# One layer of a hybrid decoder on one core: the first expert's tokens are gathered in turned form, between its first units

## The reference, cut to what matters

```
h   = rms_norm(x, ffn_norm_g)                      # 256 tokens x 1024
top_logit, top_e = top_k(h @ router_w + router_b, 4)
for each expert e:                                 # its tokens only
    gu  = xb @ w_gate_up[e] + b_gate_up[e]         # 1024 -> 2 x 1024
    act = glu * sigmoid(1.702 * glu) * (lin + 1)   # clamped at 7
    y   = act @ w_down[e] + b_down[e]              # 1024 -> 1024
x   = x + sum over e of gate * y
out = rms_norm(x, final_norm_g)
```

## Time and profile before

| | |
|---|---|
| median of three runs | 1133.32 us |
| the profiled execution, its own time | 1133.06 us |
| its span, first to last instruction | 1131.3 us |
| what lies around the span | 1.76 us |
| TensorE busy | 1083.2 us (96%) |
| DVE busy | 281.0 us (25%) |
| ACT busy | 164.9 us (15%) |
| bytes read from HBM | 430.32 MB |
| granted TensorE clock, mean | 0.998 |

### The profile page before, as it was taken

One profiled execution on the slowest core, in us unless ns is written; L12 is line 12 of the kernel. 1 busy time (PEld: TensorE's weight loads), 2 busy tenths in 40 slices (PEclk: granted clock), 3 DMA queues, 4 the chain that ended last, 5 costly groups with the idle time before them and its releaser, 6 DMA issues.

```text
span 1131.3 us, 13266 instructions
## 1 busy us (share of the span) xinstructions
PE 1083.2 (96%) x5094; PEld 466.3 (41%) x5094; DVE 281.0 (25%) x662; ACT 164.9 (15%) x347; POOL 10.2 (1%) x28
## 2 busy tenths in 40 slices
PE   7999999999999999999999999999999999999996
PEld 5578777543333333333333333333333333333333
DVE  2055532233222222222222222221111111222212
ACT  2144450210000000011000101000000000000002
POOL 0101000000000000000000000000000000000000
PEclk9999999999999999999999999999999999999999
DMA  9923652879999999999999999999999999999996
GB/s 319 332 88 149 231 216 102 353 297 419 430 431 431 431 431 432 430 432 430 433 430 433 430 433 430 432 431 432 431 431 432 430 432 430 432 430 433 430 417 266
DMA packets 47013, 431.67 MB, mean 382 GB/s; under 512 B 6256, under 2 KB 8688, under 8 KB 23408
## 3 DMA queue, kind: packets, MB, share of 16 engines
q1 hardware_dynamic: 46848, 431.12, 90.8%
q10 hardware_dynamic: 144, 0.26, 0.1%
HBM read 430.32 MB, written 1.05 MB: 381 GB/s over the span
## 4 chain that ended last, share of the span: by engine, by line
PE 59%; DMA 19%; SPq 17%; DVE 2%; issue 1%; ACT 1%; ACTq 0%
PE bank L936 23%; DMA raw<-in_w_gate_up 17%; PE bank L955 10%; PE bank L568 7%; SPq L458 7%; SPq L519 5%; SPq L461 5%; PE bank L601 4%; PE bank L572 4%; PE bank L903 3%; PE bank L870 3%; PE bank L817 2%; DMA raw<-in_w_down 1%; PE bank L622 1%; PE bank L835 0%
## 5 line engine op out<-in xcount | busy, mean ns | idle before, releaser
L936 PE MATMUL bank<-raw,xT 128*64 128x512 f32 x2048 | 462.1, 597 | 26.3 <-DMA raw<-in_w_gate_up 24.3
L936 PEld LDWEIGHTS bank<-raw,xT 128*64 128x64 f32 x2048 | 139.2, 137 | 320.6 <-issue 256.3
L955 PE MATMUL bank<-raw,actT 128*64 128x512 f32 x992 | 225.7, 596 | 0.7 <-DMA raw<-in_w_down 0.5
L955 PEld LDWEIGHTS bank<-raw,actT 128*64 128x64 f32 x992 | 68.2, 137 | 129.6 <-issue 117.1
L1555 DVE TENSOR_SCALAR gated<-cst,posc,gates 128x128 f32<-128x128 f32 x64 | 19.3, 343 | 276.4 <-PE bank L903 276.4
L1589 DVE TENSOR_TENSOR gub<-bank,bias_gu 128x512 f32<-128x512 f32 x64 | 43.9, 685 | 166.4 <-PE bank L572 166.4
L1596 DVE COPY ev_gu<-bank 128x512 f32<-128x512 f32 x32 | 22.1, 692 | 221.9 <-PE bank L936 221.9
L1221 ACT COPY ev_gu<-bank 128x512 f32<-128x512 f32 x32 | 18.7, 585 | 389.4 <-PE bank L936 389.4
L903 PE MATMUL bank<-ev,gated 64*128 64x512 f32 x248 | 61.6, 615 | 0.0
L870 PE MATMUL bank<-x_res,onehot 128*64 128x512 f32 x256 | 60.4, 592 | 0.0
L568 PE MATMUL bank<-hT,front_raw 128*128 128x256 f32 x256 | 58.9, 383 | 0.0
(11 more groups left out here) (243 smaller groups left out, 587.3 us busy)
## 6 DMA issues: line engine op xcount, KB each, us to landing
raw<-in_w_gate_up SPq DMA_DIRECT2D x124, 2048.0 KB, 41.9
raw<-in_w_down SPq DMA_DIRECT2D x60, 2048.0 KB, 43.8
front_raw<-in_w_in SPq DMA_DIRECT2D x6, 2048.0 KB, 13.8
raw<-in_w_gate_up SPq DMA_DIRECT2D x16, 512.0 KB, 17.5
raw<-in_w_down SPq DMA_DIRECT2D x16, 512.0 KB, 14.9
front_raw<-in_w_out SPq DMA_DIRECT2D x2, 2048.0 KB, 9.6
front_raw<-in_w_branch_mla SPq DMA_DIRECT2D x1, 2048.0 KB, 7.9
front_raw<-in_w_branch_dsa SPq DMA_DIRECT2D x1, 2048.0 KB, 7.9
```

Source lines behind the costliest of these rows:

```text
L936: mm = pe.matmul(GU[pair][half * SLOTS:(half + 1) * SLOTS, :], xT[:, c, b, :], w[:, at:at + BLK], start=u == 0 and k == 0, stop=last and k ...
L955: mm = pe.matmul(DN[half * SLOTS:(half + 1) * SLOTS, :], actT[:, c, u, :], w[:, at:at + BLK], start=u == 0 and c == 0, stop=u == DN_UNITS ...
```

## The change

Item 0's tokens are no longer gathered and turned. The function `first_tokens(u)` takes `xs`, with every fourth feature, as stationary operand (128 tokens x 128 features) and `onehot` as moving operand (128 tokens x 64 slots). The result has features on partitions at once. There are four groups, one for each gate-up unit, each with two chunks of 128 features and, for each, two matmuls (one a block of tokens). Each group has its own bank: 6, 3, 0 and 1. DVE multiplies each group by its part of the gain into `xT`: four instructions of 128 x 128 in place of one of 128 x 512. Groups 0 and 1 run before unit 0, group 2 between units 0 and 1, group 3 between units 1 and 2. ACT's copy of item 0's tokens, its four transposes, and the four `stay_warm` matmuls behind them are gone. TensorE's register load of `n_items` moves from before item 0 to behind item 0's last down unit, ahead of item 2. Items 1 and on are gathered as before; the counts of `gath_ps`, `gath_ev`, `xT_ps` and `xT_ok` start one lower.

```
@@ banks
+        FIRST = (B[6], B[3], B[0], B[1])
@@ TensorE
+            def first_tokens(u):
+                b, c0 = u // 2, 2 * (u % 2)
+                for k in range(2):
+                    for t in range(TT):
+                        a = b * BLK + c0 + k
+                        mm = pe.matmul(FIRST[u][:, k * SLOTS:(k + 1) * SLOTS], xs[:, t, a:a + BLK - c0 - k:4],
+                                       onehot[:, t, :], start=t == 0, stop=t == TT - 1)
+                mm.then_inc(first_ps, 1)
...
             stay_warm(WARM[2])
             pe.wait_ge(hot_ok, 1)
-            gather()
-            turn_tokens(0)
-            stay_warm(WARM[3])
-            pe.wait_ge(n_ok, 1)
-            pairs = pe.value_load(n_items[0:1, 1:2], ...) + 2
+            first_tokens(0)
+            first_tokens(1)
...
-                if u == 0:
-                    pe.wait_ge(xT_ok, i + 1)
-                    if not first:
-                        pe.wait_ge(bias_ok, 2 * i)
+                if first:
+                    pe.wait_ge(first_ok, u + 1)
+                elif u == 0:
+                    pe.wait_ge(xT_ok, i)
+                    pe.wait_ge(bias_ok, 2 * i)
...
             for u in range(GU_UNITS):
                 gate_up(0, 0, u)
+                if u < 2:
+                    first_tokens(u + 2)
...
             down(0, 0, 1)
+            pe.wait_ge(n_ok, 1)
+            pairs = pe.value_load(n_items[0:1, 1:2], ...) + 2
@@ ScalarE
-            tokens_out(0)
@@ VectorE
-            tokens_in(0)
+            for u in range(GU_UNITS):
+                b, c0 = u // 2, 2 * (u % 2)
+                dve.wait_ge(first_ps, u + 1)
+                dve.tensor_tensor(xT[:, c0:c0 + 2, b, :], FIRST[u][:, 0:2 * SLOTS].rearrange("p (c s) -> p c s", c=2),
+                                  g_tok[:, b, c0:c0 + 2].unsqueeze(2).to_broadcast([P, 2, SLOTS]), ALU.mult).then_inc(first_ok, 1)
...
             def next_tokens(i):
-                dve.wait_ge(gath_ps, i + 1)
+                if isinstance(i, int) and i == 0:
+                    dve.wait_ge(first_ps, GU_UNITS)
+                else:
+                    dve.wait_ge(gath_ps, i)
                 pick_tokens(i + 1)
```

More of the change, by code:

```diff
@@ L310, in build @@
         xT_ok = sem("xT_ok")
+        first_ps = sem("first_ps")
+        first_ok = sem("first_ok")
         sc_ps = sem("sc_ps")
@@ L872, in gather @@
                 mm.then_inc(gath_ps, 1)
+            def first_tokens(u):
[6 more added lines that the diff above has]
+                mm.then_inc(first_ps, 1)
             def turn_tokens(i):
-                pe.wait_ge(gath_ev, i + 1)
+                pe.wait_ge(gath_ev, i)
                 for c in range(4):
@@ L882, in _ @@
             pe.wait_ge(hot_ok, 1)
-            gather()
-            turn_tokens(0)
-            stay_warm(WARM[3])
-            pe.wait_ge(n_ok, 1)
-            pairs = pe.value_load(n_items[0:1, 1:2], min_val=EXPERTS // 2 - 2, max_val=EXPERTS * CHUNKS // 2 - 2) + 2
+            first_tokens(0)
+            first_tokens(1)
             def turn_scatter(i):
@@ L1018, in _ @@
             down(0, 0, 1)
+            pe.wait_ge(n_ok, 1)
+            pairs = pe.value_load(n_items[0:1, 1:2], min_val=EXPERTS // 2 - 2, max_val=EXPERTS * CHUNKS // 2 - 2) + 2
             pe.wait_ge(x1_in, 2 * TT)
@@ L1202, in tokens_out @@
             def tokens_out(i):
-                act.wait_ge(gath_ps, i + 1)
+                act.wait_ge(gath_ps, i)
                 act.copy(ev[:, :], PREP[:, :]).then_inc(gath_ev, 1)
-            tokens_out(0)
             act.wait_ge(n_ok, 1)
@@ L1572, in next_tokens @@
             def next_tokens(i):
-                dve.wait_ge(gath_ps, i + 1)
+                if isinstance(i, int) and i == 0:
+                    dve.wait_ge(first_ps, GU_UNITS)
+                else:
+                    dve.wait_ge(gath_ps, i)
                 pick_tokens(i + 1)
             def tokens_in(i):
-                dve.wait_ge(xT_ps, i + 1)
+                dve.wait_ge(xT_ps, i)
                 dve.tensor_tensor(xT[:, :, :, :], PREP[:, :].rearrange("p (c h s) -> p c h s", c=4, h=2),
```

## The result

The changed kernel is slower: median 1138.55 us of seven runs (1135.13 to 1139.31), against 1132.96 us, the median of seven runs of the kernel before (1131.37 to 1133.95). The ratio is 1.0045 with a 95% interval of 1.0034 to 1.0057. The profiled execution took 1138.69 us.

The account below looks back on a forecast made before the run. Loads were taken to bind from 259 us, their gapless start set by TensorE through item 1's start. Groups 2 and 3 add 2.20, the earlier unit 0 saves 1.87: +0.33 us, median 1133.6, range 1131.0 to 1136.0.

Parts of the forecast that it names:

- The bound: Weight loads bind from 259 us; item 1's start, not item 0's, sets when they run without gap and passes to the end.
- the other moment: Item 0's first unit ending at 237.2 us, freeing four slots, 19.5 us of loads; the alternative to item 1's first release.
- The record of 0.112 us: Matmuls of groups 0 to 3 on TensorE: 0.112 us a record, so 1.79 us for the 16 of groups 0 and 1.
- The rival that named this cause: Weights read with a stride load slowly in the groups: 0.204 us a record, +2.8 us, 1135.9; chance 0.12.
- The clock: TensorE ahead of item 0: some 0.5 us idle without the dropped warm-ups leaves the granted clock at 1.00.
- DVE's register load: Between DVE's item count and its first multiplication: 0 to 2.72 us, taken as 1.36, making DVE the new wait.
- The multiplication of 0.29: DVE's 128 x 128 multiplication from a bank ahead of unit 0, put at 0.29 us between 0.22 and 0.69.
- The 2.36 for a register load of nothing: Unit 0 of item 0 starts 2.36 us earlier if DVE's load takes nothing, since TensorE's 231.30 then counts.
- The changeover: Groups 2 and 3 between units: 0.20 us for changing over on top of 0.90 for records, 1.10 a group.
- The first four loads: Slots of units 1 to 3 free 3.48 to 4.58 us apart, a load takes 4.87, so loads run without a gap.
- The sum: Item 1 starts 2.20 - 1.87 = 0.33 us later; 1133.6 for a median, bounds -0.65 and +1.92.

Follow-up runs that it names:

- f1_between: Kernel before with 16 extra warm-up matmuls between units 0 and 1 of item 0; median +3.44 us, ratio 1.0019 to 1.0039.
- f2_item2: Kernel before with 16 extra warm-up matmuls ahead of item 2; median -0.03 us, ratio 0.9993 to 1.0012.
- e3: Changed kernel with every eighth feature instead of every fourth as stationary operand; one run, +6.83 us against the kernel before.
- g_fill: Kernel before with four start_sums matmuls moved into two waits of item 0's gather chain, and DVE's clamps put after item 1's tokens; median -0.93 us.
- g2_fill: As g_fill, but all four start_sums matmuls together under ACT's copy; -1.21 us against the kernel before, ratio 0.9984.
- f3_wide: Changed kernel with both blocks of onehot as moving operand, 128 columns instead of 64; +3.07 us against the kernel before, ratio 1.0016 to 1.0039.
- e1_row: Changed kernel with 128 neighbouring features instead of every fourth as stationary operand; -0.26 us against the kernel before, ratio 0.9988 to 1.0008.

## Why the prediction was wrong, step by step

- **The bound.** Right. Item 1's start passes to the end, work ahead of item 2 does not (`f1_between`, `f2_item2`), and ten of the thirteen profiles have a rest of 876.6 to 877.3. The three others are the second clock fall of e3, and `g_fill` and `g2_fill`, in which the other moment binds.
- **The record of 0.112 us.** This step failed. The text took the warm-ups' row, "full 128 x 128 weights", and allowed 0.127 at most in its own bounds from the bias transposes, whose stride is the same. Measured: 0.243 to 0.251. A transpose was the wrong neighbour: a transpose's load went from 140 to 204 ns with a stride, and its spacing hid that (in the kernel before, at 220.74 us, eight transposes of every eighth feature took 0.89 us, 0.111 each). A float32 matmul's load goes from 192 to 329. For groups 0 and 1 that is 3.88 us for 1.79, for groups 2 and 3 4.02 for 1.80.
- **The rival that named this cause** had the mechanism right and the size wrong. It priced a record at 0.204, the transposes' duration, and so +2.8 us. With the measured records and no clock fall the chain is 28.74 - 24.73 = 4.0 longer (`f3_wide`). A chance of 0.12 was too small for the one rule that spoke against the change, when the rows against it were of another kind of instruction.
- **The clock.** It was said to stay at full, because an idle of 2 us had not lowered it. That looked at idle time; here TensorE was never idle and the clock fell behind busy but slow matmuls. It cost 1.7 of the 1.8 us in unit 0 (5.28 against 3.58 in `f3_wide`).
- **DVE's register load.** Taken at 1.36, between 0 and 2.72; 1.03 in `e1_row`. It would have mattered: there DVE sets item 0's start. With the slow records it was hidden. The multiplication of 0.29 was right. The 2.36 for a register load of nothing should read 233.71 - 231.30 = 2.41; nothing hangs on the 0.05.
- **The changeover.** 1.10 a group with 0.20 for changing over. In `e1_row` units and groups took 3.65 + 1.04 + 3.58 + 1.04 + 7.02 = 16.33 against 13.91, so 1.21 a group.
- **The first four loads.** They were to run without a gap, with slots free 3.48 to 4.58 us apart. With the slow groups units 0, 1 and 2 end 5.6 and 5.5 us apart, more than the 4.87 of a load, and the loads sink to 213 GB/s from 246 to 247 us and to 197 from 252 to 253. The end does not feel it, since item 1's start sets it.
- **The sum** was +0.33 us. With neighbouring features `e1_row` gives +0.20 from `onehot` to item 1. That is partly luck: unit 0 started 2.23 behind `onehot`, 0.35 earlier than the 2.58 of the sum, and the two groups cost 0.22 more. These small errors aside, the size of the record, and the clock that came with it, stood between the forecast and the result.

## What to carry to other kernels

Before a stationary operand is read with a stride, look for the row of the same kind of instruction with that stride; if there is none, give the price of the unshown case real weight: here four floats apart doubled a float32 matmul's spacing while two apart were nearly free. When two engines look full, find the moment from which the transfers no longer pause, and price an edit by what it does to that moment alone. And a wait is better filled with work that must be done anyway than with warm-ups, as long as it fits the wait.

## What was not expected of the hardware

- The granted clock fell to half for about 3.5 us at the end of 16 float32 matmul records or just behind them, records with 64 moving columns at 0.23 to 0.24 us each, though TensorE counted as busy throughout. It did so in four profiles of four, and in neither of the two with 128 columns at the same spacing. It also fell in the front, at 0.52 in the stretch of 224 to 226 us of the changed kernel's profile, where nothing had changed.
- Four matmuls of 32 rows each, on four different row ranges, took 1.07 us together (8 records), and two of them alone took as long, 1.06 us (4 records, `g_fill`).
- The time from item 1's start to the end of the span repeated within 0.7 us over ten profiles on several chips, while the moment at which `onehot` was ready moved between 226.26 and 229.84 us in executions of one and the same kernel.
